# State-space scan: output matmuls with their operands exchanged, and a DRAM scratch in place of a turn on TensorE

## The reference, cut to what matters

```python
def s5_scan(u, lam_bar, b_bar, h0):
    bu = jnp.einsum('gpc,blgc->blgp', b_bar, u)        # inputs to the states
    bu = bu.at[:, 0].add(lam_bar * h0)
    ...  # states: h[l] = lam_bar * h[l-1] + bu[l]
# s5_mixer, for each of two directions (the second on the flipped sequence)
y = u * d_skip
y = y + real(einsum('gcp,blgp->blgc', c_mat, states))  # flipped back for the second
zz = gelu(y) @ w_out
```

## Time and profile before

| | us |
|---|---|
| median of 3 runs (lowest, highest) | 3198.16 (3197.5, 3198.71) |
| the profiled execution: its own time | 3196.52 |
| the profiled execution: span from first to last instruction | 3194.7 |
| the scan's eight quads, in the span | 1680.2 to 1850.9 |
| mean granted TensorE clock over the span | 0.959 |

### The profile page before, as it was taken

One profiled execution on the slowest core, in us unless ns is written; L12 is line 12 of the kernel. 1 busy time (PEld: TensorE's weight loads), 2 busy tenths in 40 slices (PEclk: granted clock), 3 DMA queues, 4 the chain that ended last, 5 costly groups with the idle time before them and its releaser, 6 DMA issues. The chain is left out here.

```text
span 3194.7 us, 48644 instructions
## 1 busy us (share of the span) xinstructions
PE 2976.4 (93%) x17528; PEld 2678.2 (84%) x17528; DVE 2033.5 (64%) x4004; ACT 1257.6 (39%) x1826; POOL 128.3 (4%) x100
## 2 busy tenths in 40 slices
PE   7967898899999999999898888988999999999997
PEld 4946798889999999988687787988899999999885
DVE  8877689864348998878736655899544344344454
ACT  3343445753333333333342234447533333333332
POOL 0000250000000000000000002500000000000000
PEclk9988899999999999999888888999999999999998
DMA  5712243664447777767612232435744444544563
GB/s 209 277 52 103 80 138 132 231 251 155 155 143 264 258 249 250 241 201 223 198 62 100 76 120 80 138 132 231 264 145 152 156 146 151 156 147 150 152 177 105
DMA packets 325055, 531.15 MB, mean 166 GB/s; under 512 B 215600, under 2 KB 218416, under 8 KB 319936
## 3 DMA queue, kind: packets, MB, share of 16 engines
q1 hardware_dynamic: 322048, 479.18, 46.3%
q10 hardware_dynamic: 2880, 50.33, 3.9%
HBM read 452.14 MB, written 77.30 MB: 166 GB/s over the span
## 5 line engine op out<-in xcount | busy, mean ns | idle before, releaser
L1967 PE MATMUL pe_s<-peer_hi,pq_uh 128*128 128x384 f32 x2304 | 788.5, 342 | 25.8 <-DVE peer_lo L163 12.6
L1969 PE MATMUL pe_s<-peer_hi,pq_ul 128*128 128x384 f32 x2304 | 777.5, 337 | 0.0
L1968 PE MATMUL pe_s<-peer_lo,pq_uh 128*128 128x384 f32 x2304 | 777.4, 337 | 0.0
L163 DVE TENSOR_TENSOR val_vl<-val_vr,val_vh 128x1024 fp32r<-128x1024 f32 x256 | 313.7, 1225 | 705.3 <-ACT val_vh L2131 705.1
L2067 ACT ACTIVATE pe_A<-pe_s 128x384 f32 (+1 forms) x256 | 126.8, 495 | 1032.6 <-PE pe_s L1969 1031.6
L1967 PEld LDWEIGHTS pe_s<-peer_hi,pq_uh 128*128 128x128 f32 x2304 | 438.3, 190 | 46.0 <-issue 25.6
L2034 PE MATMUL peer_acc<-val_vh,val_wh 128*128 128x512 f32 x1536 | 473.4, 389 | 0.7 <-DVE val_wl L163 0.7
L2034 PE MATMUL peer_acc<-val_vh,val_wl 128*128 128x512 f32 x1536 | 474.0, 390 | 0.0
L2034 PE MATMUL peer_acc<-val_vl,val_wh 128*128 128x512 f32 x1536 | 472.9, 389 | 0.0
L1968 PEld LDWEIGHTS pe_s<-peer_lo,pq_uh 128*128 128x128 f32 x2304 | 438.7, 190 | 7.8
L1969 PEld LDWEIGHTS pe_s<-peer_hi,pq_ul 128*128 128x128 f32 x2304 | 437.7, 190 | 0.0
(11 more groups left out here) (457 smaller groups left out, 3462.7 us busy)
## 6 DMA issues: line engine op xcount, KB each, us to landing
pq_ur<-in_peer_u SPq DMA_DIRECT2D x256, 512.0 KB, 3.7
val_vr<-in_peer_v SPq DMA_DIRECT2D x256, 512.0 KB, 4.4
val_gr<-gates SPq DMA_DIRECT2D x256, 192.0 KB, 4.5
val_mrow<-in_ada_rows SPq DMA_DIRECT2D x56, 512.0 KB, 4.5
gates<-gate_stg ACTq DMA_DIRECT2D x6, 4096.0 KB, 14.2
pq_ur<-in_w_query SPq DMA_DIRECT2D x32, 512.0 KB, 3.6
s_wv<-val_out SPq DMA_DIRECT2D x32, 512.0 KB, 5.3
gates<-gate_stg ACTq DMA_DIRECT2D x4, 3072.0 KB, 12.9
```

The costliest lines, as they stand in the source:

```text
L163: return nc.vector.tensor_tensor(r32(out), x, hi, ALU.subtract)
L1967: pe.matmul(o, r32(uh[:, b, k]), r32(hi[:, k]), start=k == 0, stop=False)
L1968: pe.matmul(o, r32(uh[:, b, k]), r32(lo[:, k]), start=False, stop=False)
L1969: mm = pe.matmul(o, r32(ul[:, b, k]), r32(hi[:, k]), start=False, stop=k == KC - 1)
```

## The change

It does five things, all in `s5_scan`.

1. The output matmuls exchange their operands: `MS` and `V` are stationary, and the 49 columns of `uq` or `S` move. The result lies in `yp` with (t, c) on the 128 partitions and (group, chunk) along the free side.
2. ACT copies `yp` to `Y` in one instruction instead of two, and `Y` is double.
3. The 8 turning matmuls and their wait are gone from PE. SP stores `Y` (128 partitions x 392 numbers, 196 KB) to a scratch tensor `s5_y` in DRAM, waits for it, and reads it back with 8 DMAs, one for each group, of 16 partitions each, in runs of 49 numbers, into `ys`, where features lie on partitions.
4. DVE's `outputs` reads `ys` instead of PSUM and waits for `yback`. It is moved one quad later: in quad n it does the outputs of quad n - 1, between `mask_first(n)` and `mask_second(n)`; those of quad 7 come after the final states.
5. SP's program is written out for all quads with constant addresses instead of a loop. In quad n it issues: W of n + 2 (after `product`), V of n + 2 (after `ysum`), the store of Y (after `ycopied`), then, after `ystored`, the 8 reads. `leave` waits for the last copy out of `yp` (`ycopied`) instead of `ydone`.

```diff
@@ SP @@
+                for n in range(NQ):
+                    b = n % 2
+                    if n + 2 < NQ:
+                        sp.wait_ge(product, n * 2 + 2)
+                        load(n + 2, b, 0, W, wload)
+                        sp.wait_ge(ysum, n + 1)
+                        load(n + 2, b, 1, V, vload)
+                    sp.wait_ge(ycopied, n + 2)
+                    sp.dma_start(d["s5_y"][n], Y[:, b]).then_inc(ystored[b], 16)
+                    sp.wait_ge(ystored[b], n // 2 * 16 + 32)
+                    if n >= 2:
+                        sp.wait_ge(ydone, n - 1)
+                    for g in range(QP):
+                        rows = slice(g * GC, (g + 1) * GC)
+                        sp.dma_start(ys[rows, b].rearrange("c (t k) -> c t k", t=CH),
+                                     d["s5_y"][n].rearrange("(t c) g k -> c t g k", t=CH)[:, :, g % 2 * QUAD + g // 2]).then_inc(yback[b], 16)
@@ DVE @@
-                def outputs(n):
-                    dve.wait_ge(yturned, n + 1)
-                    src = yp[:, 0, 0:CH * ROWS].rearrange("p (t k) -> p k t", t=CH)
+                def outputs(n, b, turn_):
+                    dve.wait_ge(yback[b], turn_ * 16 * QP + 16 * QP)
+                    src = ys[:, b].rearrange("p (t k) -> p k t", t=CH)
...
                     mask_first(n)
+                    if not isinstance(n, int) or n > 0:
+                        outputs(n - 1, 1 - b, turn_ - 1)
                     mask_second(n, st)
                     if more:
                         states(n + 1, 1 - b, st)
-                    outputs(n)
...
                 v.tensor_tensor(fin[:, 1], fin[:, 1], y_, ALU.add)
+                outputs(NQ - 1, 1, NQ // 2 - 1)
@@ ACT @@
                     act.wait_ge(ysum, n + 1)
-                    for gg in range(2):
-                        src = yp[0:ROWS, gg, :].rearrange("k (j t c) -> k j t c", j=QUAD, t=CH)
-                        dst = Y[:].rearrange("k t (j w) c -> k w j t c", w=2)[:, gg]
-                        nc.scalar.activation(dst, src, ACT.Copy).then_inc(ycopied, 1)
+                    act.wait_ge(ystored[b], (turn_ - b) * 16 + 16)
+                    nc.scalar.activation(Y[:, b].rearrange("p (w j) k -> p w (j k)", w=2), yp[:, :, 0:QUAD * ROWS], ACT.Copy).then_inc(ycopied, 1)
@@ PE, leave @@
-                    pe.wait_ge(ydone, n + 1)
+                    pe.wait_ge(ycopied, n + 1)
                     for j in range(QUAD):
-                        o = [yp[0:ROWS, gg, j * P:(j + 1) * P] for gg in range(2)]
+                        o = [yp[:, gg, j * ROWS:(j + 1) * ROWS] for gg in range(2)]
                         for gg in range(2):
-                            pe.matmul(o[gg], uq[:, b, 2 * j + gg, 1:1 + ROWS], MS[:, gg * QUAD + j, :], start=True, stop=False)
+                            pe.matmul(o[gg], MS[:, gg * QUAD + j, :], uq[:, b, 2 * j + gg, 1:1 + ROWS], start=True, stop=False)
...
-                                    mm = pe.matmul(o[gg], st, V[rows, b, ri, dr * QUAD + j, :], start=False, stop=dr == 1 and ri == 1)
+                                    mm = pe.matmul(o[gg], V[rows, b, ri, dr * QUAD + j, :], st, start=False, stop=dr == 1 and ri == 1)
                     mm.then_inc(ysum, 1)
-                    pe.wait_ge(ycopied, n * 2 + 2)
-                    for t in range(CH):
-                        mm = pe.matmul(yp[:, 0, t * ROWS:(t + 1) * ROWS], Y[:, t].rearrange("k g c -> k (g c)"), cx.ident[0:ROWS, 0:ROWS], start=True, stop=True)
-                    mm.then_inc(yturned, 1)
```

More of the change, by code:

```diff
@@ L2662, in s5_scan @@
         S = s.sb("S", [P, 2, 2, 2, W2])
-        Y, SF = s.sb("Y", [ROWS, CH, QP, GC]), s.sb("SF", [P, 2, NPD])
+        Y, SF = s.sb("Y", [P, 2, QP, ROWS]), s.sb("SF", [P, 2, NPD])
+        ys = s.sb("ys", [P, 2, CH * ROWS])
         tp, big, X, yp = (s.ps(n, [P, 2, 512]) for n in ("tp", "big", "X", "yp"))
@@ L2668, in s5_scan @@
         xdone, xread, hdone, sdone, sfc = (s.sem(n) for n in ("x", "x_read", "h", "s", "s_last_copied"))
-        product, masked, msdone, ysum, ycopied, yturned, ydone, zeroed = (s.sem(n) for n in (
-            "m_product", "m_first", "m_masked", "y_sum", "y_copied", "y_turned", "y_done", "zeroed"))
+        product, masked, msdone, ysum, ycopied, ydone, zeroed = (s.sem(n) for n in (
+            "m_product", "m_first", "m_masked", "y_sum", "y_copied", "y_done", "zeroed"))
+        ystored, yback = ([s.sem(f"{x}{b}") for b in range(2)] for x in ("y_stored", "y_back"))
         def rot(tab, n, k):
@@ L2681, in quads_in @@
                     emit(i * 2 + (b + 1), 1 - b, i + 1, True)
-            emit(NQ - 1, 1, 0, False)
+            emit(NQ - 1, 1, NQ // 2, False)
         with nc.Block() as block:
@@ L2688, in load @@
                     for dr in range(2):
-                        src = d["s5_wv"][bass.ds(n * 4 + (2 * kind + dr), 1)]
                         sp.dma_start(to[:, b, :, dr * QUAD:(dr + 1) * QUAD, :].rearrange("p r g m -> p r (g m)"),
-                                     src.rearrange("a p r g m -> p (a r) (g m)")).then_inc(sem[b], 16)
+                                     d["s5_wv"][n * 4 + 2 * kind + dr].rearrange("p r g m -> p r (g m)")).then_inc(sem[b], 16)
                 for b in range(2):
@@ L2768, in _ @@
                 dve.sem_inc(msdone, 1)
-                dve.sem_inc(ydone, 1)
                 dve.sem_inc(xread, 1)
@@ L2817, in _ @@
                 act.sem_inc(wtc, 2)
+                act.sem_inc(ycopied, 1)
+                for b in range(2):
+                    act.sem_inc(ystored[b], 16)
                 inputs(0, 0)
@@ L3062 @@
     d["s5_wv"] = nc.dram_tensor("s5_wv", (Builds.UNITS, P, 2, QUAD, P), F32).ap()
+    d["s5_y"] = nc.dram_tensor("s5_y", (KC, P, QP, ROWS), F32).ap()
     d["x_kept"] = nc.dram_tensor("x_kept", (P, KC, T), F32).ap()
```

## The result

The changed kernel takes 3245.51 us in the median of 4 runs (3243.88 to 3247.5), before 3198.43; the ratio is 1.0149 with a 95% interval of 1.0133 to 1.0166. It is 47 us slower, where 19 were forecast, and lies outside the range. The profiled execution's span went from 3194.7 to 3242.3 us. The scan's last DVE instruction moved from 1850.93 to 1899.21, which is 48.3 us and the whole difference: what follows is as before (7.7 us from there to the next matmul in both).

A forecast was written before the change was run, and what follows sets the result against it. PE's own length bound the scan; the new DRAM loop would, at 11.2 + 0.8 + 2.6 + 8.4 = 23.0 us a quad. Scan 166.5 against 147.9 us, +18.6, gives 3217 us, range 3187 to 3242.

The forecast's parts named there:

- The loop through DRAM: From one quad's last output matmul through copy, store, read, outputs and masks to the next's output matmuls: 23.0 us a quad.
- Read-back 11.2: From a quad's last output matmul, the last of eight reads of Y from DRAM lands 11.2 us later.
- The store behind the V loads: On SP's queue, the store of Y issued at 1.0 lands behind V's data, at 5.9 us.
- `outputs` 0.8: DVE's `outputs` after the read-back takes 0.74 us, with the wake 0.8.
- `mask_second` 2.6: On DVE, from the mask's start to the start of PE's output matmuls: 2.54, say 2.6 us.
- The exchange's own pace: Output matmuls with exchanged operands at full clock: 6.1 us a quad against 6.4 before, the long side setting the pace.
- The output matmuls' 8.4 us: Each quad's outputs on PE start at half clock after idle and take 8.4 us, 2.2 of them lost.
- the slow time after idle: PE runs 5 us at half clock after 5 to 6 us of idle before each quad's outputs.
- rival 3: PE's clock stays half through outputs, since 49 moving columns do not raise it: outputs 11.0, quad 25.6, +36.8 us; chance 0.20.
- Six steps: The six quad-to-quad steps of the scan with V loads, 23.0 us each: 138.0 us.
- the step from quad 6 to 7: Scan step without V loads, its store landing at 2.8 instead of 5.9: 19.9 us.
- PE floor of 16.9: Without the DRAM chain, PE would need 10.8 + 6.1 = 16.9 us a quad.

The follow-up runs named there:

- e4: Changed kernel with DVE's outputs(n - 1) moved behind states(n + 1) instead of ahead of mask_second(n): 3201.01 us, 1.0008 of before.
- e2: Changed kernel with output matmuls in the old operand order (49 stationary, 128 moving columns), DRAM way kept, result not the wanted one: 3222.42 us, 1.0070 of before.
- e5: Changed kernel with 49 columns streamed twice (98 moving) and outputs(n - 1) moved behind states(n + 1): 3171.98 us, 0.9927 of before.
- e9: Changed kernel with the old operand order and outputs(n - 1) behind states(n + 1), result not the wanted one: 3167.84 us, 0.9910 of before.
- e10: Changed kernel with 128 moving columns (two times 64) in the output matmuls and outputs(n - 1) behind states(n + 1): 3171.13 us, 0.9918 of before.
- e8: Changed kernel with 128 moving columns (two times 64) in each output matmul, still 128 stationary, outputs left early: 3226.65 us, 1.0095 of before.
- e3: Changed kernel with each output matmul streaming its 49 columns twice (98 moving), outputs left early: 3249.68 us, 1.0159 of before.
- e1: Changed kernel without DRAM store and reads, DVE taking ACT's copy without regrouping, result not the wanted one: 3193.92 us, 0.9986 of before.
- e6: Changed kernel with SP issuing the store of Y before the V loads of quad n + 2 instead of behind them: 3220.65 us, 1.0078 of before.

## Why the prediction was wrong

The sign, the place and the mechanism of the chain were right. By its own steps, forecast and measured:

- The loop through DRAM: right. e4 takes the wait out of it and gains 44.5 us.
- Read-back 11.2: 11.8 in quad 2 (1761.3 to 1773.12), 11.6 to 12.0 in quads 3 to 5, 13.2 in the first two (1705.03 to 1718.27 in the first). Of the 0.6 in quad 2, 0.5 is the store's issue, 1.5 behind the last output matmul instead of 1.0, since the two V issues took 1.17. In quad 0 the eight reads' issues took 5.06 instead of 3.63, one of them 1.82; in quad 1 they took 3.63, but DVE woke 3.0 behind the last of them instead of 1.7. Why, stays open. The store behind the V loads (4.9), the reads' issue (3.63 against 3.2 to the last one's start) and landing (1.9) are as forecast.
- `outputs` 0.8: 0.9 (1773.12 to 1774.03). `mask_second` 2.6: 2.6 (1774.03 to 1776.65). The exchange's own pace: 6.4 us at full clock (1.60 for each pair of groups in quad 0 against 1.58 before), where I took 6.1; the long side sets the pace, as the earlier trace rows said, and nothing is gained.
- **The output matmuls' 8.4 us: this step failed.** I took the slow time after idle, 5 us, from matmuls with 128 moving columns, and carried it over to matmuls with 49. For the old order the number is near (e2: 8.3 to 8.9, with a slow stretch of 5.3 in quad 3). For the new ones the clock never came back within the outputs: 11.44 in five of the seven quads. This is rival 3, which got 0.20. Its price of 3235 lacked three things: 2.5 us in the outputs (11.4 for its 11.0), 2.3 in quad 0, and 6.7 in the way through DRAM. It had its row: before, the slow stretch stood right behind the turn of Y, whose moving operand has 49 columns too. I set that aside for the 1.17 us of idle beside it. The row did not decide between the two, and after the turn of quad 1, with the same wait, the local product took 2.12, at full clock. Likewise quad 0, which I left untouched, lost the clock after just 0.54 us of idle and ended 2.3 us later than I had it.

The parts add up. Six steps took 1867.73 - 1705.03 = 162.7 us against 138.0; the step from quad 6 to 7 took 22.7 against 19.9, the tail 8.8 against 8.9, quad 0's outputs another 2.3. That is 29.7 more than the forecast's 18.6, together the 48.3 measured. By cause, 20.7 of the 29.7 stand in the output matmuls of the seven steps (79.5 us together against 7 x 8.4 = 58.8) and 2.3 in quad 0, of which the clock is 1.7 (8.14 us for its outputs against 6.4 at full clock), the pace taken too fast 0.3 and a later start 0.2. Nearly all of the remaining 6.7 is the read-back; 0.1 for each `outputs` and the tail make the rest.

The forecast of a PE floor of 16.9 without the chain was near e5's 15.9 and e9's 15.7, but these held the clock throughout; with the chain gone and the clock lost it was 20.2 (e4). The change's idea, the turn off TensorE, was worth 0.7 to 0.8% with the wanted result (e5, e10) and 0.9% by the bound of e9. It was lost twice: by a wait placed in front of the masks, and by output matmuls with 49 moving columns, through which the clock did not hold.

## What to carry to other kernels

When the operands of small matmuls are exchanged, read the granted clock as well as the pace: where the stationary side already sets the pace, streaming the columns twice costs little (6.4, 6.6 and 6.8 us for the outputs with 49, 98 and 128 columns at full clock) and can keep the clock, as in e5 and e10. A consumer of a DRAM round trip belongs behind everything in its engine's order that the producer's next round waits for. Carry the cost of a start at half clock over only from matmuls of the same shape: e2 and e8 came back within the outputs, the changed kernel and e3 did not.

## What the runs showed of the hardware that was not expected

- PE busy in 11.00 of 11.00 us, with the granted clock at 0.50 throughout (the row of quad 3): busy time in the profile does not tell whether the clock holds. The Trainium skill, TensorE: Matmul & The Clock Gate, "What's actually happening", says that the gate goes by how busy PE has been recently. By the busy share of this row the clock should have been full, and it was not; the measurement decides.
- With 128 stationary columns and nearly the same pace (1.60, 1.68 and 1.73 us for a pair of groups): outputs with 49 moving columns lost the clock after 0.5 us of idle (e1, e4). With 98 it held after that, but did not come back after 2.6 to 7.6 us of idle (e5's last quad, e3). With 128 it came back after 5.7 to 7.7 us of idle (e8). No other widths were tried.
- Small reads behind 1 MB of loads on one queue landed in 3.4 us instead of 1.9, and the store ahead of them in 1.9 instead of 4.9 (e6): on this one queue the order of issue decided, also between a store and loads.
